# Feed-forward blocks: one more slab by seven products in three of four, and the next stage's input work pulled ahead of the weight split

## The chip, the cores and the metric

The kernel runs on one core of one Trainium2 chip, as one program. The metric is device time in microseconds (us) from one execution. Engines: TensorE (PE; its weight loads PEld), VectorE (DVE), ScalarE (ACT), GpSimd (POOL) and SyncE (SP), which issues the DMAs.

## The reference, cut to what matters

Two blocks follow one another, each two layers deep, on x of 512 tokens by 1024 channels, all float32. Each layer of the first block holds two feed-forward blocks, with a mixer (stick-breaking attention beside a gated delta rule) and a cross attention between them; the second block's layers are attention with a gated embedding.

```python
def swiglu_ffn(x, w_in, w_out):
    gate, up = jnp.split(x @ w_in, 2, axis=-1)
    return (jax.nn.silu(gate) * up) @ w_out

for l in range(DEPTH):                     # DEPTH = 2, D_FF = 2816
    h = h + 0.5 * swiglu_ffn(rms_norm(h, ffn1_norm[l]), ffn1_w_in[l], ffn1_w_out[l])
    h = h + hybrid_mixer(rms_norm(h, mix_norm[l]), ...)
    h = h + memory_cross_attention(rms_norm(h, xattn_norm[l]), rms_norm(mem, mem_norm[l]), ...)
    h = h + 0.5 * swiglu_ffn(rms_norm(h, ffn2_norm[l]), ffn2_w_in[l], ffn2_w_out[l])
```

So there are four feed-forward blocks, called here the first (ffn1 of layer 0) to the fourth (ffn2 of layer 1).

## The kernel before, in words

**Numbers in two parts.** Each float32 operand is split into a high part (rounded to the matmul's own type, made by ScalarE as a copy) and a low part (what is left, made by VectorE as a subtraction). One product of the mathematics is three matmuls: high by high, high by low, low by high (line 346).

**Slabs.** Weights stream from memory in slabs of 128 partitions. A slab of an input projection is 2048 wide and holds 8 chunks of channels for two groups of 128 output columns. Three raw buffers hold slabs; SyncE loads slab g when slab g-3 was used. ScalarE makes the high part of slab g (`high`, line 314) into one of two buffers once slab g-2 was used; VectorE makes the low part (`low`, line 321) in place. While TensorE works on slab s, the other engines prepare slab s+2 as far as they can.

**A feed-forward block** (class `Ffn`) has two halves. Each half has 11 input slabs (one hidden chunk of 128 each: a gate product and an up product) and then 8 "deep" slabs, which multiply the 11 hidden chunks by w_out into one chunk of 128 channels of h each. Input slabs are of two kinds:

- *plain*: 8 chunks by 2 outputs by 3 matmuls of 512 columns (48 matmuls). VectorE evicts both outputs times the row's norm factor (line 3523), ScalarE applies silu, VectorE multiplies (3538), ScalarE makes the high part of the hidden chunk (3430) and VectorE the low part (3541).
- *seven*: the product as 2 by 2 blocks with seven block products in place of eight (Strassen's form, Winograd's variant), 7 by 4 by 3 = 84 matmuls of 256 columns (line 3365). Its units run in the order A11, S1, S2, A12, S3, S4, A22. Before it VectorE makes three sums of weight blocks (3595 to 3600), and ScalarE and VectorE split them: `vector_first` (3605) gives the low part that A11 waits for, `vector_rests` (3611) and `vector_second` (3616) the others. During it VectorE adds partial products in a "join" (3624): unit S3 waits for the first join, unit A22 for the second.

**Blocks of x.** The sevens need x itself in blocks: seven tiles of 128x1024, from h times gain times the norm factor (`vector_row`, 3656, two rows of four instructions), four sums (3635 to 3641), seven high copies on ScalarE (3506) and seven low parts on VectorE (3647). The first A11 of a block waits for all seven low parts. Before, five slabs are plain in the second to fourth block and the work on x is spread over slabs 0 to 3 (`x_from` 0); in the first block six are plain and it is spread over slabs 1 to 4 (`x_from` 1). `vector_x(s, 0)` stands behind the slab's eviction, `vector_x(s, 1)` behind the product of silu and up.

**The slab ahead of the first seven** (`vector_enter`, evictions on line 3560) prepares slab s+2 between its own steps.

**What sets the order.** Each engine runs one fixed program, written by the loops over slabs, and stays in order; semaphores tie the engines. `tensor_plain` waits for the split slab, for two free banks of four (those of slab s-2) and in slab 0 for each chunk of the new x. The norm's matmuls (`norm_tensor`, line 464) stand in slab 0 ahead of chunk `NORM_AT`, in the first block in slab 1. `NextX` makes the next stage's x chunk by chunk from h: high (ScalarE, 415), square (422), low (VectorE, 433) and sum of squares (443). `LoadX` starts the program: it issues the loads and runs `WARM` float32 matmuls of ones (line 1076), while the first chunks of x and of slab 0 come in and are split.

Of the kernel before, what the change touches and what calls it, by code (L numbers as in the profile page):

```python
# [628 lines left out]
class Project(Stage):  # L629
# [42 lines left out]
    def scalar(self, act):  # L672
        for s, (r, i) in enumerate(self.slabs):
            for side in self.sides:
                side.scalar(act, s)
            if s == 0 and self.norm is not None:
                self.norm.norm_scalar(act)
            if len(self.jobs[s]) == 2:
                r.evac.scalar(self.k, act, self.jobs[s], 0, i)
            if (s or not self.first) and not (self.split_later and s == len(self.slabs) - 1):  # L680
                self.k.high(act, self.g0 + s + 2)
            if self.jobs[s]:
                r.evac.scalar(self.k, act, self.jobs[s], len(self.jobs[s]) - 1, i)

    def vector(self, dve):
        k = self.k
        for s, (r, i) in enumerate(self.slabs):
# [9 lines left out]
            if (s or not self.first) and not (self.split_later and s == len(self.slabs) - 1):  # L697
                k.low(dve, self.g0 + s + 2)
            if self.jobs[s]:
                r.evac.finish(k, dve, self.jobs[s], len(self.jobs[s]) - 1, i)  # L700

# [309 lines left out]
class LoadX(Stage):  # L1011

    WARM = 12
# [2174 lines left out]
class Ffn(Stage):  # L3188
# [6 lines left out]
    NORM_AT = 5  # L3195
# [3 lines left out]
    def __init__(self, k, name_at, x, gain, next_x, sides=(), first=False):  # L3199
# [5 lines left out]
        self.plain, self.x_from = (6, 1) if first else (5, 0)  # L3205
# [197 lines left out]
    def scalar(self, act):  # L3403
        k = self.k
        for s, slab in enumerate(self.slabs):
# [8 lines left out]
            if slab.kind == "plain":  # L3414
                act.wait_ge(k.bank_free, slab.jobs[0].n + 1)
                a = self.hidden(slab.j, F32)[0]
                k.nc.scalar.activation(a, a, ACT.Silu).then_inc(k.act_done, 1)
            if ahead is None:
# [12 lines left out]
            elif slab.j[1]:  # L3431
                act.wait_ge(k.bank_free, slab.jobs[0].n + 1)
                self.next_x.scalar(act, slab.j[0])
# [75 lines left out]
    def vector(self, dve):  # L3509
        k, nc = self.k, self.k.nc  # L3510
        for s, slab in enumerate(self.slabs):
# [5 lines left out]
            if now is not None and slab.kind == "plain":  # L3517
                self.vector_enter(dve, s)
                continue
            if slab.kind == "plain":  # L3520
# [7 lines left out]
            self.vector_x(dve, s, 0)  # L3528
# [13 lines left out]
            elif slab.j[1]:  # L3542
                self.next_x.vector(dve, slab.j[0])
# [83 lines left out]
    def vector_x(self, dve, s, part):  # L3627
# [9 lines left out]
        elif at == (1, 1):  # L3637
# [4 lines left out]
        rest = {(2, 0): ((self.A11, 1), (self.S3, 4)), (2, 1): ((self.S1, 5), (self.S2, 6), (self.A12, 2)),  # L3642
                (3, 0): ((self.S4, 3), (self.A22, 7))}
# [297 lines left out]
```

## Time and profile before

| | |
|---|---|
| median of 3 runs | 3074.25 us (3070.44 to 3074.66) |
| profiled execution | 3071.89 us |
| its span in the trace | 3070.1 us |
| mean granted clock of TensorE | 0.999 |
| TensorE busy | 3037.7 us, 99% of the span |
| VectorE busy | 1990.5 us, 65% |
| ScalarE busy | 1498.1 us, 49% |
| DMA | 25.1% of 16 engines, 90 GB/s |

TensorE is on nearly all of the chain that ended last (92% of it). A duration in a timeline row is an instruction's own; successive instructions of one engine overlap by some hundredths of a microsecond, so the distance between two starts is what one of them costs in a queue. A row with xN merges N instructions. The bracket behind a row is the idle time ahead of it and what ended that.

### The profile page before, as it was taken

Reading aid. Unit: us, or ns where it says so; the run is one execution under the profiler, and the core shown is the slowest. Engines: PE = TensorE matmul, PEld = TensorE weight load, DVE = VectorE, ACT = ScalarE, POOL = GpSimd, SP = SyncE. Lnnn points to the kernel's source line nnn. Section 1 sums busy time; section 2 is a strip of 40 time slices with the busy share of each in tenths; the row PEclk is TensorE's granted clock in tenths of the full one; section 3 lists DMA queues with packets and bytes.
Section 4 is the critical chain, followed back from the end, with each engine's and each line's share of the span. In section 5 each row is a group of like instructions: output and inputs, shape, how many; then the busy total and the mean of one; then the engine's idle time right before and its main releaser. Section 6 shows DMA issues by size and latency. Waiting matters only on the chain.

```text
span 3070.1 us, 45342 instructions
## 1 busy us (share of the span) xinstructions
PE 3037.7 (99%) x19178; PEld 2603.2 (85%) x19178; DVE 1990.5 (65%) x2741; ACT 1498.1 (49%) x2083; POOL 150.3 (5%) x158
## 2 busy tenths in 40 slices
PE   9999999999999999999999999999999999999999
PEld 7999887888789998989887788789998886888777
DVE  7667439855584866758447855576675568554774
ACT  5444436553453544435335653454444558454673
POOL 0000000300000000000000200000000006000150
PEclk9999999999999999999999999999999999999999
DMA  4232321132122322232221122122222220222202
GB/s 158 99 115 99 115 72 66 43 124 83 69 97 90 112 97 102 97 116 96 104 83 69 56 85 109 55 96 97 109 98 101 94 83 29 81 104 83 83 31 88
DMA packets 49545, 275.29 MB, mean 90 GB/s; under 512 B 5312, under 2 KB 8896, under 8 KB 26304
## 3 DMA queue, kind: packets, MB, share of 16 engines
q1 hardware_dynamic: 49344, 272.40, 25.1%
q8 instruction: 152, 2.49, 0.3%
q14 instruction: 49, 0.40, 0.0%
HBM read 270.28 MB, written 2.10 MB: 89 GB/s over the span
## 4 chain that ended last, share of the span: by engine, by line
PE 92%; DVE 5%; ACT 2%; issue 1%; DMA 0%; POOL 0%; DVEq 0%; SPq 0%; ACTq 0%; POOLq 0%
PE banks L346 61%; PE banks L3365 22%; PE banks L2612 1%; PE banks L2653 1%; ACT weights L2993 1%; DVE weights L3041 1%; PE banks L1682 1%; PE banks L1832 1%; PE banks L1648 0%; PE banks L1668 0%; ACT slab_hi L314 0%; DVE weights_turned L3062 0%; PE banks L1845 0%; PE banks L3784 0%; PE banks L1703 0%
## 5 line engine op out<-in xcount | busy, mean ns | idle before, releaser
L314 ACT ACTIVATE slab_hi<-slab_raw 128x2048 fp32r<-128x2048 f32 (+2 forms) x207 | 351.7, 1699 | 638.9 <-PE banks L346 615.0
L346 PE MATMUL banks<-x_hi,slab_hi 128*128 128x512 f32 x1488 | 589.1, 396 | 2.5 <-DVE x_lo L433 2.1
L346 PE MATMUL banks<-x_hi,slab_lo 128*128 128x512 f32 x1488 | 580.2, 390 | 0.0
L346 PE MATMUL banks<-x_lo,slab_hi 128*128 128x512 f32 x1488 | 580.0, 390 | 0.0
L321 DVE TENSOR_TENSOR slab_lo<-slab_raw,slab_hi 128x2048 fp32r<-128x2048 f32 (+2 forms) x203 | 409.6, 2018 | 181.6 <-ACT slab_hi L314 181.4
L3365 PE MATMUL banks<-x_blocks_hi,x_area_parts 128*128 128x256 f32 x1736 | 399.4, 280 | 0.0
L346 PE MATMUL banks<-hidden_parts,slab_hi 128*128 128x512 f32 x1280 | 394.3, 389 | 0.0
L346 PEld LDWEIGHTS banks<-x_hi,slab_hi 128*128 128x128 f32 x1488 | 279.7, 188 | 67.9 <-issue 8.7
L346 PEld LDWEIGHTS banks<-x_lo,slab_hi 128*128 128x128 f32 x1488 | 279.9, 188 | 59.5 <-issue 2.9
L346 PEld LDWEIGHTS banks<-x_hi,slab_lo 128*128 128x128 f32 x1488 | 279.6, 188 | 58.9
L3365 PE MATMUL banks<-x_blocks_hi,slab_lo 128*128 128x256 f32 x1072 | 299.2, 279 | 0.0
L3365 PEld LDWEIGHTS banks<-x_blocks_hi,x_area_parts 128*128 128x128 f32 x1736 | 296.7, 188 | 0.8 <-issue 0.5
L346 PEld LDWEIGHTS banks<-hidden_parts,slab_hi 128*128 128x128 f32 x1280 | 239.6, 188 | 49.3
L3365 PE MATMUL banks<-x_blocks_lo,x_area_parts 128*128 128x256 f32 x980 | 273.6, 279 | 0.0
L346 PE MATMUL banks<-hidden_parts,slab_lo 128*128 128x512 f32 x640 | 249.1, 389 | 0.0
L3365 PE MATMUL banks<-x_blocks_hi,slab_hi 128*128 128x256 f32 x784 | 219.5, 280 | 0.0
L3365 PE MATMUL banks<-x_blocks_lo,slab_hi 128*128 128x256 f32 x784 | 218.9, 279 | 0.0
L3365 PEld LDWEIGHTS banks<-x_blocks_hi,slab_lo 128*128 128x128 f32 x1072 | 201.3, 188 | 0.0
L3365 PEld LDWEIGHTS banks<-x_blocks_lo,x_area_parts 128*128 128x128 f32 x980 | 183.5, 187 | 0.2
L3577 DVE SCALAR_TENSOR_TENSOR h<-banks,h 128x512 f32<-128x512 f32 x64 | 44.2, 691 | 214.5 <-PE banks L346 214.5
L3365 PEld LDWEIGHTS banks<-x_blocks_hi,slab_hi 128*128 128x128 f32 x784 | 147.1, 188 | 0.2 <-issue 0.2
L3365 PEld LDWEIGHTS banks<-x_blocks_lo,slab_hi 128*128 128x128 f32 x784 | 146.8, 187 | 0.0
(458 smaller groups left out, 5466.0 us busy)
## 6 DMA issues: line engine op xcount, KB each, us to landing
slab_raw<-slabs SPq DMA_DIRECT2D x195, 1024.0 KB, 4.8
slab_raw<-slabs SPq DMA_DIRECT2D x64, 704.0 KB, 4.0
slab_raw<-slabs SPq DMA_DIRECT2D x16, 640.0 KB, 3.8
h<-xT SPq DMA_DIRECT2D x8, 256.0 KB, 5.8
memory<-memT SPq DMA_DIRECT2D x2, 1024.0 KB, 5.4
out<-h SPq DMA_DIRECT2D x7, 256.0 KB, 4.9
constants<-con SPq DMA_DIRECT2D x1, 1284.5 KB, 9.8
slab_raw<-slabs SPq DMA_DIRECT2D x4, 256.0 KB, 5.2
```

The source lines that it names most:

```text
L314: self.nc.scalar.activation(self.wh[:, g % self.HIGHS, 0:w], self.raw[:, g % self.RAWS, 0:w], ACT.Copy).then_inc(self.hi_ready, 1)
L321: self.nc.vector.tensor_tensor(self.wl[:, g % self.RAWS, 0:w], self.raw[:, g % self.RAWS, 0:w], self.wh[:, g % self.HIGHS, 0:w].bitcast(F3 ...
L346: mm = self.nc.tensor.matmul(out, left[a], right[c], start=start and n == 0, stop=stop and n == 2)
L1682: mm = nc.tensor.matmul(ps[64 * c:64 * c + 64, 2, b * P:S], v[:, b, (2 * p + c) * SB_DIM:(2 * p + c + 1) * SB_DIM], self.prob[:, at:at + n ...
L1832: mm = nc.tensor.matmul(self.product_bank(g)[rows, u - 8 * g, :], self.lm[n][rows, u, :], self.d[rows, u, :], start=True, stop=True, skip_ ...
L2612: mm = nc.tensor.matmul(self.scores_of(u), self.q[:, 2 * h + c, tb * P:(tb + 1) * P], self.kt[:, 2 * h + c, :], start=c == 0, stop=c == 1)
L2653: mm = nc.tensor.matmul(ps[:, self.out_banks[h][c], :], self.v[:, b, (2 * h + c) * P:(2 * h + c + 1) * P], self.pt[:, h % 2, b, :], start= ...
L2993: ins = nc.scalar.activation(w, w, ACT.Exp, scale=-1.0, bias=self.col(self.nm, tb, c), accum_out=self.col(self.sm, tb, c))
L3041: ins = nc.vector.tensor_tensor_reduce(self.weights(u, c)[:, at], self.bank(u, c)[:, at], self.table(u // self.UNITS)[:, S - (tb + 1) * P: ...
L3365: mm = self.k.nc.tensor.matmul(out, left[a], right[c], start=start and n + a + c == 0, stop=n == self.BLOCK - 1 and a == 1, skip_group_che ...
L3577: k.nc.vector.scalar_tensor_tensor(out=h, in0=k.ps[:, job.bank, :], scalar=0.5, in1=h, op0=ALU.mult, op1=ALU.add) \
```

## The change

Five edits:

1. `plain` goes from 5 to 4 in the second, third and fourth feed-forward block: hidden chunk 4 becomes a seven. The first block stays at 6.
2. In all four blocks `vector_x(s, 0)` stands ahead of the slab's eviction where s > `x_from`, and the seven low parts of x go over two slabs (four and three) in place of three slabs (two, three and two).
3. At a projection's last slab, and at each deep slab of the second half, the next x (high, square, low, sum) stands ahead of the split of slab s+2.
4. `NORM_AT` goes from 5 to 3.
5. `WARM` goes from 12 to 20.

```diff
--- before.py
+++ after.py
@@ -677,10 +677,13 @@
                 self.norm.norm_scalar(act)
             if len(self.jobs[s]) == 2:
                 r.evac.scalar(self.k, act, self.jobs[s], 0, i)
-            if (s or not self.first) and not (self.split_later and s == len(self.slabs) - 1):
+            last, more = s == len(self.slabs) - 1, s or not self.first
+            if more and not last:
                 self.k.high(act, self.g0 + s + 2)
             if self.jobs[s]:
                 r.evac.scalar(self.k, act, self.jobs[s], len(self.jobs[s]) - 1, i)
+            if more and last and not self.split_later:
+                self.k.high(act, self.g0 + s + 2)
 
     def vector(self, dve):
         k = self.k
@@ -694,10 +697,13 @@
                 r.evac.vector(k, dve, self.jobs[s], n, i)
                 if n == 0 and len(self.jobs[s]) == 2:
                     r.evac.finish(k, dve, self.jobs[s], n, i)
-            if (s or not self.first) and not (self.split_later and s == len(self.slabs) - 1):
+            last, more = s == len(self.slabs) - 1, s or not self.first
+            if more and not last:
                 k.low(dve, self.g0 + s + 2)
             if self.jobs[s]:
                 r.evac.finish(k, dve, self.jobs[s], len(self.jobs[s]) - 1, i)
+            if more and last and not self.split_later:
+                k.low(dve, self.g0 + s + 2)
 
     def tensor(self, pe):
         k = self.k
@@ -1010,7 +1016,7 @@
 
 class LoadX(Stage):
 
-    WARM = 12
+    WARM = 20
 
     def __init__(self, k, x, sources):
         self.k, self.x, self.sources = k, x, sources
@@ -3192,7 +3198,7 @@
 
 
     HALF, BLOCK, COLS = FC // 2, KC // 2, S // 2
-    NORM_AT = 5
+    NORM_AT = 3
     UNITS, LAST = 7, FC + KC
     A11, S1, S2, A12, S3, S4, A22 = range(UNITS)
 
@@ -3202,7 +3208,7 @@
         for side in self.sides:
             side.of = self
         at_in, at_out = name_at
-        self.plain, self.x_from = (6, 1) if first else (5, 0)
+        self.plain, self.x_from = (6, 1) if first else (4, 0)
         self.slabs = []
         self.g0 = k.claim("slab", 2 * (self.HALF + KC))
         for half in range(2):
@@ -3415,6 +3421,9 @@
                 act.wait_ge(k.bank_free, slab.jobs[0].n + 1)
                 a = self.hidden(slab.j, F32)[0]
                 k.nc.scalar.activation(a, a, ACT.Silu).then_inc(k.act_done, 1)
+            if slab.kind == "deep" and slab.j[1]:
+                act.wait_ge(k.bank_free, slab.jobs[0].n + 1)
+                self.next_x.scalar(act, slab.j[0])
             if ahead is None:
                 if self.more(s):
                     k.high(act, slab.g + 2)
@@ -3428,9 +3437,6 @@
                 else:
                     act.wait_ge(k.bank_free, slab.jobs[1].n + 1)
                 k.nc.scalar.activation(self.hidden(slab.j)[0], self.hidden(slab.j, F32)[1], ACT.Copy).then_inc(k.hh_ready, 1)
-            elif slab.j[1]:
-                act.wait_ge(k.bank_free, slab.jobs[0].n + 1)
-                self.next_x.scalar(act, slab.j[0])
             self.scalar_x(act, s, 1)
             if now is not None:
                 self.scalar_seed(act, now)
@@ -3517,6 +3523,8 @@
             if now is not None and slab.kind == "plain":
                 self.vector_enter(dve, s)
                 continue
+            if s > self.x_from:
+                self.vector_x(dve, s, 0)
             if slab.kind == "plain":
                 for job, to in zip(slab.jobs, self.hidden(slab.j, F32)):
                     dve.wait_ge(job.sem, job.value)
@@ -3525,7 +3533,10 @@
                 self.vector_hidden(dve, s)
             else:
                 self.vector_add(dve, s)
-            self.vector_x(dve, s, 0)
+                if slab.j[1]:
+                    self.next_x.vector(dve, slab.j[0])
+            if s <= self.x_from:
+                self.vector_x(dve, s, 0)
             if ahead is not None:
                 self.vector_sums(dve, ahead)
             elif self.more(s):
@@ -3539,8 +3550,6 @@
                 self.vector_x(dve, s, 1)
                 dve.wait_ge(k.hh_ready, self.n0 + slab.j + 1)
                 nc.vector.tensor_tensor(hl, product, hh.bitcast(F32), ALU.subtract).then_inc(k.hl_ready, 1)
-            elif slab.j[1]:
-                self.next_x.vector(dve, slab.j[0])
             if now is not None:
                 self.vector_join(dve, now, 0)
             if ahead is not None:
@@ -3639,8 +3648,8 @@
             nc.vector.tensor_tensor(t2, b22, t1, ALU.subtract).then_inc(self.x_made.sem, 1)
             dve.wait_ge(*self.x_made.at(5))
             nc.vector.tensor_tensor(t4, b21, t2, ALU.subtract).then_inc(self.x_made.sem, 1)
-        rest = {(2, 0): ((self.A11, 1), (self.S3, 4)), (2, 1): ((self.S1, 5), (self.S2, 6), (self.A12, 2)),
-                (3, 0): ((self.S4, 3), (self.A22, 7))}
+        rest = {(2, 0): ((self.A11, 1), (self.A12, 2), (self.S4, 3), (self.S3, 4)),
+                (2, 1): ((self.S1, 5), (self.S2, 6), (self.A22, 7))}
         for u, n in rest.get(at, ()):
             dve.wait_ge(*self.x_hi.at(n))
             dve.wait_ge(*self.x_made.at(6))
```

VectorE's program in the second feed-forward block, from slab 1's eviction on, before (`hidden<-banks` is an eviction, `x_blocks` the work on x, `slab_lo ... 128x2048` the low part of plain slab s+2):

```order
L3523 TENSOR_TENSOR hidden<-banks,rstd 128x512 x2
L3635 TENSOR_TENSOR x_blocks<-x_blocks 128x1024
L3636 TENSOR_TENSOR x_blocks<-x_blocks 128x1024
L321 TENSOR_TENSOR slab_lo<-slab_raw,slab_hi 128x2048
L3538 TENSOR_TENSOR hidden<-hidden 128x512
L3639 TENSOR_TENSOR x_blocks<-x_blocks 128x1024
L3641 TENSOR_TENSOR x_blocks<-x_blocks 128x1024
L3541 TENSOR_TENSOR hidden_parts<-hidden,hidden_parts 128x512
L3523 TENSOR_TENSOR hidden<-banks,rstd 128x512 x2
L3647 TENSOR_TENSOR x_blocks_lo<-x_blocks,x_blocks_hi 128x1024 x2
L321 TENSOR_TENSOR slab_lo<-slab_raw,slab_hi 128x2048
L3538 TENSOR_TENSOR hidden<-hidden 128x512
```

The same stretch now (lines of the changed kernel):

```order
L3644 TENSOR_TENSOR x_blocks<-x_blocks 128x1024
L3645 TENSOR_TENSOR x_blocks<-x_blocks 128x1024
L3531 TENSOR_TENSOR hidden<-banks,rstd 128x512 x2
L321 TENSOR_TENSOR slab_lo<-slab_raw,slab_hi 128x2048
L3549 TENSOR_TENSOR hidden<-hidden 128x512
L3648 TENSOR_TENSOR x_blocks<-x_blocks 128x1024
L3650 TENSOR_TENSOR x_blocks<-x_blocks 128x1024
L3552 TENSOR_TENSOR hidden_parts<-hidden,hidden_parts 128x512
L3656 TENSOR_TENSOR x_blocks_lo<-x_blocks,x_blocks_hi 128x1024 x4
L3531 TENSOR_TENSOR hidden<-banks,rstd 128x512 x2
L3604 TENSOR_TENSOR first_sums<-slab_raw 128x512
L3605 TENSOR_TENSOR slab_raw<-slab_raw 128x4x128
```

The work on x now stands ahead of each eviction, and the first seven's sums follow slab 2's eviction; the low parts of plain slab 4 are gone.

VectorE in the same block, from the last sum of the first seven (slab 5) to what its first unit waits for (`slab_lo<-slab_raw,hidden_parts`, the first of the two), before:

```order
L3600 TENSOR_TENSOR first_sums<-slab_raw,first_sums 128x512
L3538 TENSOR_TENSOR hidden<-hidden 128x512
L3541 TENSOR_TENSOR hidden_parts<-hidden,hidden_parts 128x512
L3605 TENSOR_TENSOR slab_lo<-slab_raw,hidden_parts 128x1024
L3611 TENSOR_TENSOR first_sums_parts<-first_sums,hidden_parts 128x1536
L3616 TENSOR_TENSOR slab_lo<-slab_raw,hidden_parts 128x1024
L3560 TENSOR_TENSOR hidden<-banks,rstd 128x512 x2
```

And now, for slab 4:

```order
L3609 TENSOR_TENSOR first_sums<-slab_raw,first_sums 128x512
L3549 TENSOR_TENSOR hidden<-hidden 128x512
L3656 TENSOR_TENSOR x_blocks_lo<-x_blocks,x_blocks_hi 128x1024 x3
L3552 TENSOR_TENSOR hidden_parts<-hidden,hidden_parts 128x512
L3614 TENSOR_TENSOR slab_lo<-slab_raw,hidden_parts 128x1024
L3620 TENSOR_TENSOR first_sums_parts<-first_sums,hidden_parts 128x1536
L3625 TENSOR_TENSOR slab_lo<-slab_raw,hidden_parts 128x1024
L3569 TENSOR_TENSOR hidden<-banks,rstd 128x512 x2
```

Three low parts of x now stand between the product and the first seven's own low parts.

ScalarE at the seam ahead of the second feed-forward block (last slab of the projection ahead of it), before:

```order
L314 ACTIVATE slab_hi<-slab_raw 128x2048
L415 ACTIVATE x_hi<-h,params 128x512
L422 ACTIVATE h_squares<-h 128x512
L474 ACT_TABLE_LOAD
L474 ACTIVATE rstd<-banks 128x512
```

And now:

```order
L415 ACTIVATE x_hi<-h,params 128x512
L422 ACTIVATE h_squares<-h 128x512
L314 ACTIVATE slab_hi<-slab_raw 128x2048
L474 ACT_TABLE_LOAD
L474 ACTIVATE rstd<-banks 128x512
```

The last chunk's high part and square moved ahead of the slab's high part; VectorE's side moves in the same way.

## Rows read from the trace of the kernel before

**Rows 1.** the page's first part: busy time, share of the span, instructions

```profile
PE 3037.7 (99%) x19178; PEld 2603.2 (85%) x19178; DVE 1990.5 (65%) x2741; ACT 1498.1 (49%) x2083; POOL 150.3 (5%) x158
```

**Rows 2.** chain of waits in order of time: start, us, what

```profile
8.09 18.21 PE banks L346 x72
...
76.16 49.88 PE banks L3365 x420
...
846.07 47.65 PE banks L346 x210
893.72 59.80 PE banks L3365 x504
```

**Rows 3.** waits of TensorE, whole span: us in total, times, longest

```profile
PE banks L2910 <- ACT weights_turned L3003: 9.1, 18, 0.6
...
PE banks L346 <- DVE x_lo L433: 2.1, 1, 2.1
```

**Rows 4.** timeline of TensorE from the program's start: start, us, instruction

```profile
1.10 4.92 PE L1076 MATMUL banks<-ones 128*128 128x128 f32 x24 [1.10 <-DVE ones L1059]
...
4.68 1.35 PE L1076 MATMUL banks<-ones 128*128 128x128 f32 x8
```

**Rows 5.** windows: busy us of each engine, PEclk, DMA

```profile
8.00:10.00 2.00, 1.91 (x6) 1.57 (x7) 1.51 (x3) 1.57 (x3) 0.00 (x0) 0.67 1.02 362
10.00:12.00 2.00, 2.00 (x7) 1.52 (x6) 1.86 (x4) 1.69 (x4) 0.00 (x0) 0.50 1.09 420
```

**Rows 6.** timeline of VectorE, first feed-forward's first half

```profile
19.18 5.46 DVE L443 TENSOR_TENSOR sum_of_squares<-sum_of_squares,h_squares 128x512 f32<-128x512 f32 x7
...
43.61 1.28 DVE L3523 TENSOR_TENSOR hidden<-banks,rstd 128x512 f32<-128x512 f32 x2
...
70.85 0.69 DVE L3538 TENSOR_TENSOR hidden<-hidden 128x512 f32<-128x512 f32 x1
...
81.23 0.42 DVE L3624 TENSOR_TENSOR banks<-banks,fifth_product 128x256 f32<-128x256 f32 x1
```

**Rows 7.** timeline of ScalarE, the same stretch

```profile
27.19 0.60 ACT L474 ACTIVATE rstd<-banks 128x512 f32<-128x512 f32 x1 [0.36 <-PE banks L464]
```

**Rows 8.** timeline of VectorE, second feed-forward's first half

```profile
849.63 1.30 DVE L3523 TENSOR_TENSOR hidden<-banks,rstd 128x512 f32<-128x512 f32 x2 [5.62 <-PE banks L346]
...
859.55 0.69 DVE L3523 TENSOR_TENSOR hidden<-banks,rstd 128x512 f32<-128x512 f32 x1
...
861.72 1.22 DVE L3635 TENSOR_TENSOR x_blocks<-x_blocks 128x1024 f32<-128x1024 f32 x1
...
863.99 2.28 DVE L321 TENSOR_TENSOR slab_lo<-slab_raw,slab_hi 128x2048 fp32r<-128x2048 f32 x1
...
869.19 0.68 DVE L3541 TENSOR_TENSOR hidden_parts<-hidden,hidden_parts 128x512 fp32r<-128x512 f32 x1
...
890.75 1.23 DVE L3605 TENSOR_TENSOR slab_lo<-slab_raw,hidden_parts 128x1024 fp32r<-128x1024 f32 x1 [0.26 <-ACT hidden_parts L3476]
892.12 1.76 DVE L3611 TENSOR_TENSOR first_sums_parts<-first_sums,hidden_parts 128x1536 fp32r<-128x1536 f32 x1 [0.15 <-ACT hidden_parts L3480]
...
894.94 1.28 DVE L3560 TENSOR_TENSOR hidden<-banks,rstd 128x512 f32<-128x512 f32 x2
...
898.79 0.42 DVE L3624 TENSOR_TENSOR banks<-banks,fifth_product 128x256 f32<-128x256 f32 x1
```

**Rows 9.** timeline of ScalarE, the same stretch

```profile
860.98 0.61 ACT L3417 ACTIVATE hidden<-hidden 128x512 f32<-128x512 f32 x1
861.50 1.90 ACT L314 ACTIVATE slab_hi<-slab_raw 128x2048 fp32r<-128x2048 f32 x1
```

**Rows 10.** timeline of VectorE, the seam ahead of the second feed-forward

```profile
838.44 0.69 DVE L901 SCALAR_TENSOR_TENSOR h<-banks,h 128x512 f32<-128x512 f32 x1 [2.57 <-PE banks L346]
...
843.32 0.68 DVE L443 TENSOR_TENSOR sum_of_squares<-sum_of_squares,h_squares 128x512 f32<-128x512 f32 x1
```

**Rows 11.** timeline of TensorE at the same seam

```profile
845.05 1.02 PE L464 MATMUL banks<-sum_of_squares,ones 128*128 128x512 f32 x2
```

## The prediction

> **What bounds the kernel now.** I read four views in this order. First the busy times [rows 1]: TensorE works 99% of the span, VectorE 65%, so over the whole only TensorE's own work counts. Then the chain of waits [rows 2]: the reader is to see that plain slabs and sevens follow each other as one stretch of TensorE, with nothing between. Third TensorE's list of waits [rows 3]: no line of a feed-forward block or of a seam stands in it, except one wait of 2.1 us at the start. Last the timelines of VectorE and ScalarE in the stretch that the change touches [rows 6 to 9]. The average hides what they show: ahead of a block's first seven VectorE has hardly a pause. The question is whether it can do the same work one slab earlier.
>
> Durations come from one execution of 3071.89 us (span 3070.1, so 1.8 lies around it). The median shown is 3074.25, which is 2.36 more; I add that at the end.
>
> **What a slab costs.** 210 matmuls of 512 columns take 47.65, 0.2269 each, so a plain slab of 48 takes 10.89. 504 of 256 columns take 59.80, 0.1187 each, so a seven of 84 takes 9.97 [rows 2]. Each moved slab gives 0.92, three give 2.77. Within a seven the unit S3 starts after 4 units of 12, that is 5.70 after its start.
>
> **Edits 1 and 2, second to fourth block.** TensorE would want slab 4 at 893.72 - 10.89 = 882.83. VectorE must by then have finished the first low part of slab 4's seven. In steps from slab 0's eviction at 849.63, durations being distances between starts [rows 8]:
> - to slab 1's eviction as before: 9.92 (859.55)
> - x(1, 0), two sums, now ahead of the eviction: 863.99 - 861.72 = 2.27
> - eviction 1.21 (1.30 for the pair, less overlap)
> - low part of 2048, product, two sums: 869.19 - 863.99 = 5.20
> - low part of the hidden chunk 0.61
> - four low parts of x, at 2.27 / 2 each: 4.54
> - slab 2's eviction 1.21, then the first seven's sums. From an eviction at 894.94 to the join at 898.79 are 3.85; less 1.21 this gives 2.64 for the sums
> - product 0.61, three low parts of x 3.41, hidden low part 0.61, and the seven's first low part 1.22 (890.75 to 892.12, less 0.15 idle).
>
> The sum is 33.45, done at 883.08 without a single pause. That is already 0.25 late. One pause I expect: before, ScalarE's silu starts at 860.98 and the high part of 2048 at 861.50, for 1.90, so VectorE's low part can start at 863.4 and starts at 863.99 [rows 8, 9]. Now the eviction comes 2.27 later. It ends at 859.55 + 2.27 for the first output; silu starts at about 862.5, the high part at 863.06, and it ends at 864.96. VectorE would be at its low part at 863.03, so it idles 1.97. The first low part is done at 885.05 and TensorE starts at 885.10: a stall of 2.27.
>
> A second one follows. Behind the first low part VectorE has the rest (2.82 from 892.12 to 894.94), the eviction with sums (3.85) and the join's first instruction (0.42). From the first low part's start, 883.83: 883.83 + 1.13 + 2.82 + 3.85 + 0.42 = 892.05. S3 waits for this and is wanted at 885.10 + 5.70 = 890.80: a stall of 1.30. Then both are in step, with VectorE the shorter one as in the sevens now.
>
> Per block 2.27 + 1.30 - 0.92 = 2.65, times three 7.95. What is queued behind the wait on TensorE is the whole seven, and nothing else can use the time. The bounds of this term: with the pause hidden 0.25 + 0.05 + 1.30 - 0.92 = +0.68 per block; with no stall at all -0.92; with a second such pause at slab 2 it could reach +4.6. I take 2.65, for each of its steps has a row of the same instruction.
>
> **First block, edits 2 and 5.** Plain slabs stay six. The 12 products of ones leave two records each: 24 take 4.92, 0.205 each [rows 4]. Eight more are 16 records: 3.28, ending at 6.02 + 3.28 = 9.30 at that rate. The first 16 took 3.58 (4.68 - 1.10), 0.224 each, and at half of that the addition ends at 7.81. The real work can start at 8.09 [rows 2]. Now TensorE idles 2.1 ahead of it [rows 3], and the granted clock is 0.67 and then 0.50 in the four microseconds behind [rows 5], that is down to the lower of its two levels (1.2 GHz). So the 72 matmuls take 18.21 in place of 72 x 0.2269 = 16.34. If the ones fill the gap, 1.87 are gained; but the norm's matmuls behind them need the sums of squares, which end at 19.18 + 5.46 = 24.64 [rows 6], while 72 matmuls at full speed end at 24.43. TensorE would be ahead by 26.13 - 24.70 = 1.43, the norm factor by only 0.36, since ScalarE waits just 0.36 for it (its table load is on the way) [rows 7].
>
> No row shows that the clock stays up through 8:00 to 12:00 if the ones go on; that the last eight records took 1.35, 0.169 each against 0.224, shows it rising under them [rows 4].
>
> But VectorE sets this block's first seven too. With x(2, 0) ahead of the eviction, in the same steps from slab 1's eviction at 43.61 - 0.36 = 43.25 [rows 6]: x(2, 0) to 45.52, eviction 46.73, a pause for ScalarE's high part to 48.70, 5.20 to 53.90, hidden 54.51, four low parts 59.04, eviction 60.25, high part and low part of slab 5 to 64.51. TensorE wants slab 5 at 63.84 and stalls some 0.7. Then product, three low parts, hidden low part, eviction, sums: 72.89. Before, from that point (70.85) to the join (81.23) are 10.38. Now the join ends at 72.89 + 10.38 + 0.42 = 83.69 and S3 starts at 83.74. Before, it started at 76.16 + 5.70 = 81.86. This block costs +1.88. VectorE sets it, so the warm-up's gain is lost: without it the block would be 0.36 later. Bounds: -1.43 (no stall) to +2.8 (the ones end at 9.30 and the stalls stand).
>
> **Edits 3 and 4.** At a seam TensorE waits for nothing now. The norm's matmuls at 845.05 [rows 11] move up by two chunks of six: to 842.33. The sum of squares ends at 844.00 now [rows 10], too late for that; with x in front it is h at 838.44 + 0.69 = 839.13, then high, square and sum at about 0.6 to 0.7 each, 841.1: 1.2 to spare. The split of the slab behind it comes 2.4 later but is due only at the start of slab 1, 5 us after. In the deep slabs the extra steps ahead of the split take 2 of some 7.5 us. I cost both at 0; if edit 3's cover failed, edit 4 would stall up to 1.7 per seam.
>
> **The sum.** 3071.89 + 1.88 + 7.95 = 3081.72. Plus 2.36, rounded down for the pauses that partly overlap: **3083.0**.
>
> **Rivals.**
> A, VectorE has the reserve after all, and nothing stalls: not slower. Place: the wait ahead of the first seven. It decides if the first low part is done by 882.83, that is if 33.45 + 1.97 shrink to 33.20. For it: TensorE waits nowhere in these blocks now, and VectorE is at 65%. Against it: the sum of rows is over it even without a pause. Time: -2.77 - 1.43 = -4.2, 3070.0.
>
> B, the pause of 1.97 isn't there (ScalarE's silu comes between, or other waits shift) but the work is too much: +0.68 x 3 + 1.88 = +3.9, 3078.
>
> C, the stalls bring the clock down. For it: after the one idle stretch of 2.1 us in the trace the clock went to 0.67 and 0.50 [rows 5], and 1.87 were lost. Three stalls of 2.27 could each cost up to 1.87 more; since a slower TensorE reaches S3 later, up to 1.30 of that hides in the second stall. So +0.6 to +1.9 a block, 3085 to 3089, say 3087. Against it: that idle stretch followed only 5 us of work, these follow hundreds. The Trainium skill, "TensorE: Matmul & The Clock Gate", section "Why this matters for your kernels", warns only of long idle gaps between bursts of matmuls; by that rule the three stalls would cost nothing beyond themselves and C falls away. The row at the start agrees with it only in part: there the clock fell behind a gap no longer than these.
>
> D, the longer run of ones doesn't do what it says: the clock falls all the same. That takes 0.36 off the gain as long as VectorE sets the block and 1.43 in case A (then 3071.5). Nothing in the rows excludes it; it goes with each case, and gets no chance of its own.
>
> **How the numbers follow.** A difference of 0.2% (6.1 us) is about what can be told from no change: 3068.1 to 3080.4. Forecast 0.52, own range 3079 to 3087; B 0.20; C 0.15; A 0.13. Slower takes 0.45 of the forecast, 0.05 of B and C whole: 0.65. Faster has a third of A: 0.04. The rest is 0.31. The range of 3072 to 3090 leaves out most of A and what lies above C.
>
> **What would show it.** In the profile after, VectorE idles some 2 us for the slab's high part in slab 1 of three blocks and not again up to the first seven. TensorE waits there for VectorE's low part of slab 4, about 2.3, three times, and for the join about 1.3. The first block shows stalls of 0.7, then 1 to 1.5. From 8 to 12 the granted clock is 1.00. No wait at the norm's matmuls, except at the first block. I am wrong if the first seven starts without a wait, if the waits are there but the clock in the seven behind them is under 1.00, or if a norm or a deep slab shows a wait.

## The result and the profile after

The changed kernel takes 3083.43 us (median of 6 runs, 3081.71 to 3085.5), the kernel before 3074.32 in the same comparison (3070.44 to 3075.14). The ratio is 1.0033, 95% interval 1.002 to 1.0046: slower, by 9 us. The forecast was 3083.0. That it agrees with the median to 0.4 is partly luck, for the runs of one kernel spread over 4 or more; the parts below show which terms were right by more than luck.

The page's first part of the changed kernel, span 3082.6 (before [rows 1]):

```profile
PE 3041.2 (99%) x19302; PEld 2611.1 (85%) x19302; DVE 2004.4 (65%) x2759; ACT 1505.3 (49%) x2098; POOL 150.3 (5%) x158
```

The shares are those of before. The reader who looks only here finds nothing. TensorE's waits do show it (us in total, times, longest); none of these lines was in the list of before:

```profile
PE banks L3371 <- DVE slab_lo L3614: 7.8, 4, 2.3
...
PE banks L3371 <- DVE banks L3633: 2.4, 2, 1.2
...
PE banks L346 <- DVE slab_lo L321: 0.7, 1, 0.7
```

Line 3371 is the seven. `slab_lo L3614` is the low part of its first unit, `banks L3633` the join ahead of S3. Each wait of three blocks for the low part is 2.35, and the fourth, in the first block, is 0.77. S3 waits 1.25 in the first block, 1.12 in the second and not at all in the third and fourth. The start's wait of 2.1 [rows 3] is gone from the list, and the windows that showed the clock's fall [rows 5] now read 1.00 in the column PEclk, the third from the right:

```profile
8.00:10.00 2.00, 2.00 (x13) 1.74 (x13) 1.75 (x4) 1.86 (x3) 0.00 (x0) 1.00 1.00 344
10.00:12.00 2.00, 2.00 (x11) 1.65 (x10) 0.98 (x3) 0.94 (x2) 0.00 (x0) 1.00 1.10 425
```

VectorE in the second block (timeline: start, us, instruction, idle ahead), which answers to [rows 8]:

```profile
853.51 1.30 DVE L3531 TENSOR_TENSOR hidden<-banks,rstd 128x512 f32<-128x512 f32 x2 [5.08 <-PE banks L346]
...
865.70 1.28 DVE L3531 TENSOR_TENSOR hidden<-banks,rstd 128x512 f32<-128x512 f32 x2
868.89 2.29 DVE L321 TENSOR_TENSOR slab_lo<-slab_raw,slab_hi 128x2048 fp32r<-128x2048 f32 x1 [1.91 <-ACT slab_hi L314]
...
887.70 1.22 DVE L3614 TENSOR_TENSOR slab_lo<-slab_raw,hidden_parts 128x1024 fp32r<-128x1024 f32 x1
...
895.49 0.42 DVE L3633 TENSOR_TENSOR banks<-banks,fifth_product 128x256 f32<-128x256 f32 x1
```

From the first eviction to the end of the seven's first low part are 888.92 - 853.51 = 35.41; the prediction had 33.45 + 1.97 = 35.42. The one pause behind the first eviction is 1.91, for ScalarE's high part. The same pause is found in the first block, twice.

Where TensorE's time went can be read off the chain of waits, by the start of the first 264 matmuls behind each block's first sevens (start, us, what). After:

```profile
128.56 59.87 PE banks L346 x264
...
960.09 59.87 PE banks L346 x264
...
1306.69 59.87 PE banks L346 x264
...
2135.92 59.87 PE banks L346 x264
```

Before, the same places:

```profile
126.04 59.87 PE banks L346 x264
...
953.52 59.87 PE banks L346 x264
...
1297.32 59.87 PE banks L346 x264
...
2123.58 59.87 PE banks L346 x264
```

The offsets are +2.52, +6.57, +9.37, +12.34. Taking off what each block starts with (0, 3.88, 6.46, 9.40, from the same chain), the four blocks cost 2.52, 2.69, 2.91 and 2.94. The forecast had 1.88 and three times 2.65. The step from 2.52 to 3.88 lies between the blocks, in the gated delta rule's stage, and steps of this size come and go there with the code unchanged (run 11).

### The profile page after: what moved, and what is told of

Same layout as the page of the kernel before. It is cut to its first block, busy times and chain, and to the rows that moved or that the text cites. A ratio compares the mean times of both kernels' runs of the same rounds, so it can differ in the third digit from the quotient of the medians.

```text
span 3082.6 us, 45635 instructions
## 1 busy us (share of the span) xinstructions
PE 3041.2 (99%) x19302; PEld 2611.1 (85%) x19302; DVE 2004.4 (65%) x2759; ACT 1505.3 (49%) x2098; POOL 150.3 (5%) x158
## 4 chain that ended last, share of the span: by engine, by line
PE 86%; DVE 9%; ACT 3%; issue 2%; DMA 0%; SPq 0%; DVEq 0%; POOL 0%; ACTq 0%; POOLq 0%
PE banks L346 54%; PE banks L3371 22%; PE banks L2618 1%; PE banks L2659 1%; DVE x_blocks_lo L3656 1%; ACT slab_hi L314 1%; ACT weights L2999 1%; DVE weights L3047 1%; PE banks L1688 1%; DVE x_blocks L3665 1%; PE banks L1838 1%; DVE hidden L3531 0%; DVE slab_lo L321 0%; PE banks L1654 0%; PE banks L1674 0%
## 5 line engine op out<-in xcount | busy, mean ns | idle before, releaser
L346 PE MATMUL banks<-x_hi,slab_hi 128*128 128x512 f32 x1440 | 569.9, 396 | 1.2 <-DVE slab_lo L321 0.7
L346 PE MATMUL banks<-x_hi,slab_lo 128*128 128x512 f32 x1440 | 560.9, 389 | 0.0
L346 PE MATMUL banks<-x_lo,slab_hi 128*128 128x512 f32 x1440 | 560.8, 389 | 0.0
L3371 PE MATMUL banks<-x_blocks_hi,x_area_parts 128*128 128x256 f32 x1772 | 408.9, 279 | 0.0
L3371 PE MATMUL banks<-x_blocks_hi,slab_lo 128*128 128x256 f32 x1120 | 314.2, 281 | 0.0
L3371 PE MATMUL banks<-x_blocks_hi,slab_hi 128*128 128x256 f32 x868 | 243.4, 280 | 0.0
L3371 PE MATMUL banks<-x_blocks_lo,slab_hi 128*128 128x256 f32 x868 | 242.3, 279 | 0.0
L3371 PEld LDWEIGHTS banks<-x_blocks_hi,slab_lo 128*128 128x128 f32 x1120 | 211.8, 189 | 0.0
L3371 PEld LDWEIGHTS banks<-x_blocks_hi,slab_hi 128*128 128x128 f32 x868 | 162.8, 188 | 0.7 <-issue 0.7
L3371 PEld LDWEIGHTS banks<-x_blocks_lo,slab_hi 128*128 128x128 f32 x868 | 162.6, 187 | 0.0
```

Source lines behind the costliest of these rows:

```text
L346: mm = self.nc.tensor.matmul(out, left[a], right[c], start=start and n == 0, stop=stop and n == 2)
L3371: mm = self.k.nc.tensor.matmul(out, left[a], right[c], start=start and n + a + c == 0, stop=n == self.BLOCK - 1 and a == 1, skip_group_che ...
```

## The experiments

In every run a block's cost is the shift of TensorE against the first profile of before between that block's beginning and the end of its first sevens, as just shown. That is finer than the medians: runs of one kernel differ by 4 to 9 us, in good part for a reason that comes last. Ratios are to the kernel before on the same chip, with 95% intervals.

**1. Five plain slabs in the three blocks, all else changed.**

```diff
-        self.plain, self.x_from = (6, 1) if first else (4, 0)
+        self.plain, self.x_from = (6, 1) if first else (5, 0)
```

> The changed kernel with five plain slabs again in the second to fourth block; everything else as changed. My theory (VectorE is late for a seven that comes one slab sooner; with five plain slabs it has a slab of TensorE's time more) expects no wait ahead of the first seven in these three blocks, though VectorE's pause of about 1.9 in slab 1 stays, and the loss of the first block alone: before + 2.4, 3076.7, some 6.7 under the changed kernel. The rival (the order of x ahead of the evictions costs by itself in every block) expects stalls there too and 3080 or more.

Measured: 3076.83, ratio 1.0014 (1.0005 to 1.0023). Blocks +2.47, +0.82, +0.79, +0.77. No wait ahead of a later block's first seven. But S3 waits in all four:

```profile
PE banks L3371 <- DVE banks L3633: 3.3, 4, 1.2
```

So the first seven's stall comes from taking a slab away. Edit 2 costs by itself as well, 0.8 per block, where I had expected nothing, and the four blocks together lose 4.85 where I had expected 2.4 (that the median is near the 3076.7 expected is chance: before ran at 3071.75 beside it). VectorE now pauses 1.9 for ScalarE's high part in slab 1 and again in slab 2, and its join starts at 901.82, 3.03 later than before, while TensorE is only 2.23 later there. S3 had 0.2 to spare [rows 2, 8] and cannot absorb that. Whether the order of x or the gathering of its low parts in two slabs weighs more was not separated.

**2. Evictions ahead of x again, four plain slabs.**

```diff
-            if s > self.x_from:
-                self.vector_x(dve, s, 0)
...
-            if s <= self.x_from:
-                self.vector_x(dve, s, 0)
+            self.vector_x(dve, s, 0)
```

> The changed kernel with the work on x behind the eviction in every slab, as before; four plain slabs and the low parts of x over two slabs stay. My theory expects VectorE's pauses of 1.9 to go in all four blocks, the stall ahead of the three first sevens to fall from 2.35 to 0.3 to 0.5, that at S3 to stay at 1.1 to 1.3, and the first block to lose under 0.5: 3074.3 + 3 x (0.4 + 1.2 - 0.92) = 3076.3, 7 under the changed kernel. The rival (VectorE's amount of work alone sets it, the pause is time that it has anyway) expects the stalls as they are and 3083.

Measured: 3080.65, ratio 1.0025 (1.0016 to 1.0034). Blocks -1.46, +3.52, +3.54, +3.53. My expectation was wrong: in the first block it came, and more (-1.46, the ones included), in the others the stall grew to 2.93. The pauses show why (VectorE's timeline):

```profile
859.38 0.69 DVE L3529 TENSOR_TENSOR hidden<-banks,rstd 128x512 f32<-128x512 f32 x1 [0.88 <-PE banks L346]
...
870.26 0.69 DVE L3529 TENSOR_TENSOR hidden<-banks,rstd 128x512 f32<-128x512 f32 x1 [1.52 <-PE banks L346]
```

The pause of 1.91 for ScalarE is gone, but the eviction that now stands in front waits for TensorE to end the slab, twice, 2.40 together. These two pauses are those of the kernel before, to the hundredth, as its own timeline has them between the rows of [rows 8]: 0.88 ahead of slab 1's second eviction, and

```profile
872.00 0.69 DVE L3523 TENSOR_TENSOR hidden<-banks,rstd 128x512 f32<-128x512 f32 x1 [1.52 <-PE banks L346]
```

The wait at S3 that I had expected did not show. Behind each of the three stalls the granted clock fell (0.65 and 0.50 in the two windows from 884 to 888, second block), so TensorE came to S3 later. For four plain slabs the changed order is the better of the two, by 0.6 to 0.8 a block; a part of that can be the clock, which fell in all three blocks here and in two of three there.

**3. The seams and the norm alone** (edits 3 and 4 on the kernel before; the projections' part of edit 3 goes in as in the change's diff).

```diff
-    NORM_AT = 5
+    NORM_AT = 3
...
+            if slab.kind == "deep" and slab.j[1]:
+                act.wait_ge(k.bank_free, slab.jobs[0].n + 1)
+                self.next_x.scalar(act, slab.j[0])
```

> The kernel before with edits 3 and 4 alone: the next x ahead of the split at the seams, and the norm ahead of chunk 3. My theory costs them at nothing: no wait at the norm, none at a deep slab, 3074.3 within 1. The rival (the split that now comes later is late for the slab behind the seam) expects a wait of TensorE for a slab's low part, 0.5 or more at each of some seams, 3076 or more.

Measured: 3072.17 against 3071.75, ratio 1.0001 (0.9992 to 1.001). Blocks 2 to 4: within 0.02 of nothing; no wait at a norm or deep slab of the later blocks. Costed rightly at nothing.

**4. Twenty products of ones alone**, on the kernel before.

```diff
-    WARM = 12
+    WARM = 20
```

> The kernel before with 20 products of ones in place of 12. The granted clock stays at 1.00 in the first 12 us and TensorE is some 1.4 earlier at the first norm. My theory expects VectorE to give nearly all of this back at the first seven's S3, where the join ends only 0.2 before TensorE wants it: a gain of 0.2 to 0.4, 3074.0. The rival (TensorE's lead lasts) expects 1.4 to 1.9 less than before: 3072.6.

Measured: 3070.85, ratio 0.9994 (0.9985 to 1.0002), which the timing cannot tell from no change. In the trace the first block is 1.33 earlier than in the first profile of before, and the lead lasts to the block's end: the rival was right on that. How much of it the ones give is less sure, since the same code as before was 0.87 earlier in one execution (run 11). VectorE's evictions had waited for TensorE there, by this row and one like it at 54.44 in the trace of before:

```profile
65.32 0.69 DVE L3523 TENSOR_TENSOR hidden<-banks,rstd 128x512 f32<-128x512 f32 x1 [0.51 <-PE banks L346]
```

An earlier TensorE lets VectorE go earlier too, so the slack of 0.2 at S3 is not used up. In this profile the lead is lost behind the block, in the gated delta rule's stage (1.34, granted clock 0.57 from 604 to 608, as in run 11), and both spans are 3070.1.

**5. Each part of the work on x one place earlier**, evictions in front, and ScalarE's high copies of x with them; the first block as before, edits 3 to 5 as changed.

```diff
+            if s == 0 and not self.first:
+                self.vector_row(0)
...
+            steps = {(0, 0): 1, (0, 1): 2, (1, 0): 3}
+            rest = {(1, 1): ((self.A11, 1), (self.A12, 2), (self.S4, 3), (self.S3, 4)),
+                    (2, 1): ((self.S1, 5), (self.S2, 6), (self.A22, 7))}
```

> Four plain slabs in three blocks, evictions ahead of x, and in these three blocks each part of the work on x one place earlier: the first row ahead of slab 0's eviction, where VectorE idles 5.08 and the norm factor is ready 3.5 before it, then row, sums, sums, four low parts in slab 1 and three in slab 2. The first block has its order of before; edits 3 to 5 as changed. My theory, corrected by the last runs (an eviction cannot run before TensorE ends its slab, and the first seven's sums cannot before slab 2 ends at 875.9 in the changed kernel's clock): behind that point 0.61 + 2.64 + 0.61 + 3.41 + 0.61 + 1.22 = 9.1, done at 885.0, TensorE wants it at 886.7: no stall; the join ends at 892.0 and S3 is wanted at 892.4: none. So three times -0.92 and a little from the ones: before - 3. The rival (VectorE's amount of work ahead of the first seven sets it, wherever it stands) expects the stalls of about 3 per block to stay, before + 6 to 8.

Measured: 3070.43 against 3072.36, ratio 0.9988 (0.9979 to 0.9997): faster than before. Blocks -1.03, -0.50, -0.58, -0.54. The row of x stands in the pause ahead of the first eviction:

```profile
844.84 2.74 DVE L3674 SCALAR_TENSOR_TENSOR x_blocks<-h,params,rstd 128x512 f32<-128x512 f32 x4 [1.56 <-ACT rstd L479]
848.29 1.37 DVE L3534 TENSOR_TENSOR hidden<-banks,rstd 128x512 f32<-128x512 f32 x2 [0.71 <-PE banks L346]
```

The same four plain slabs, the same work, and no stall ahead of the first seven; S3 keeps 0.31 each, where I had expected none, so a block gains 0.5 to 0.6 and not 0.92. So the amount of work was not the bound. What bound was that it stood behind waits.

**6. ScalarE's high part ahead of silu**, all else changed.

```diff
+                if ahead is None and self.more(s):
+                    k.high(act, slab.g + 2)
                 act.wait_ge(k.bank_free, slab.jobs[0].n + 1)
...
-                if self.more(s):
+                if self.more(s) and slab.kind != "plain":
                     k.high(act, slab.g + 2)
```

> The changed kernel, but ScalarE makes a plain slab's next high part ahead of silu in place of behind it, so that VectorE's low part needn't wait for it. My theory (the pause of 1.91 in slab 1, two of them in the first block, passes on to the first seven in full) expects 3 x 1.9 + 2.3 less than the changed kernel: its stalls 3.5 per block fall to 1.6, the first block loses under 0.5, before + 2.5. The rival (the pause is only changed into a wait for TensorE's evictions, as in the run with the evictions ahead) expects the stalls of 2.35 to stay above 2, and under 2 gained.

Measured: 3073.21 against 3072.36, ratio 1.0 (0.9991 to 1.0009). Blocks -2.61, +0.84, +0.88, +0.85. Waits:

```profile
PE banks L3371 <- DVE banks L3635: 3.0, 3, 1.0
...
PE banks L3371 <- DVE slab_lo L3616: 1.4, 3, 0.5
```

This is the cleanest test of the forecast's main step. The pause is gone from the second block's timeline, the stall ahead of the first seven falls from 2.35 to 0.47, by the 1.9 of the pause, and the one at S3 stays at 1.01. The pause is not VectorE's spare time. No fall of the clock follows these shorter stalls.

**7. The first block in its order of before**, all else changed.

```diff
-            if s > self.x_from:
+            if s > self.x_from and not self.first:
...
-            if s <= self.x_from:
+            if s <= self.x_from or self.first:
...
+        if self.first:
+            rest = {(2, 0): ((self.A11, 1), (self.S3, 4)), (2, 1): ((self.S1, 5), (self.S2, 6), (self.A12, 2)),
+                    (3, 0): ((self.S4, 3), (self.A22, 7))}
```

> The changed kernel with the order of before in the first block alone (x behind the evictions, low parts over three slabs). My theory: the first block's three stalls (0.74, 0.77, 1.25) go, about 2.4 less than the changed kernel, and the three others stay as they are. The rival (they come from the longer run of ones, or TensorE's lead only turns into another wait) expects the sum of that block's waits to stay above 1.5.

Measured: 3080.12, ratio 1.002 (1.0011 to 1.0029). Blocks -1.58, +2.72, +2.98, +2.97. All waits of the first block are gone, which is 4.1 against the changed kernel; I had expected 2.4, and left out that the ones' 1.4 comes through once VectorE no longer sets the block.

**8. The norm at 3 alone**, on the kernel before.

```diff
-    NORM_AT = 5
+    NORM_AT = 3
```

> The kernel before with NORM_AT 3 alone, the next x still behind the split. My theory: the last sum of squares ends at 844.00 in the trace of before, and TensorE now wants it at 842.33, so it waits 1.7 at each of three seams, 5 in all, and nothing later gives it back: before + 5. The rival (TensorE's norm may come late, but the norm factor and the first evictions come no later than before, and banks are free) says the same stall is there but 1 or more is given back at a later wait: before + 2 or less.

Measured: 3078.84, ratio 1.002 (1.001 to 1.0029). The later blocks' shift is +1.88, +1.84, +1.84; TensorE waits at each seam:

```profile
PE banks L464 <- DVE sum_of_squares L443: 4.7, 3, 1.6
```

Edit 3 is thus what makes edit 4 free. Nothing is given back: the shift is some 0.3 above the wait of 1.57 each.

**9. As 5, with the sum for t2 between the two evictions of slab 1.**

```diff
+                    if s == n == 1 and not self.first:
+                        self.vector_t2(dve)
```

> The run with x one place earlier, and the sum for t2 moved in between the two evictions of slab 1, where VectorE idled 1.26 for TensorE. My theory expects the whole chain behind it 1.1 earlier, the 0.31 wait at S3 gone, and so 0.92 gained per block in place of 0.55: before - 1.3 (the ones) - 2.8 = before - 4.1. The rival (the wait at S3 is set by what stands behind the first seven's sums, which wait for slab 2's end anyway) expects the 0.31 to stay and before - 3.

Measured: 3068.8 against 3073.31, ratio 0.9985 (0.9976 to 0.9994), the fastest of all by its blocks (the two ratios' intervals, of 5 and 9, overlap). Blocks -1.22, -1.11, -1.14, -1.15. The wait at S3 is gone, and VectorE's timeline shows t2 where the pause was:

```profile
857.68 0.68 DVE L3536 TENSOR_TENSOR hidden<-banks,rstd 128x512 f32<-128x512 f32 x1
858.29 1.21 DVE L3673 TENSOR_TENSOR x_blocks<-x_blocks 128x1024 f32<-128x1024 f32 x1
859.63 0.69 DVE L3536 TENSOR_TENSOR hidden<-banks,rstd 128x512 f32<-128x512 f32 x1
```

A block gains 1.12, and not 0.92, because the price of the added seven was taken too high. Nothing waits here, and seven sevens take (chain of waits)

```profile
881.36 69.57 PE banks L3371 x588
```

against 59.80 for six before [rows 2]: 9.77 for the one more, where a plain slab takes 10.89. The forecast's 9.97 was the average of the six, which holds some 0.4 of short losses: the sevens of the second half run at 108.83 for 924, 0.1178 each, and those six at 0.1187.

**10. The changed kernel with 12 products of ones.**

```diff
-    WARM = 20
+    WARM = 12
```

> The changed kernel with 12 products of ones again. The prediction said that VectorE sets the first block and the ones give it 0.36 at most; with the ones alone the kernel of before gained 1.3 in its trace. My theory: in the changed kernel ScalarE's table load and VectorE's chain behind it start at the same time with either number, so the first block ends within 0.4 of where it ends now (first deep slab at 128.4). The rival (the ones' 1.3 comes through here as well) expects it at 129.7.

Measured: 3083.81, ratio 1.0033 (1.0022 to 1.0044). First block +2.44, where the changed kernel has +2.52: the ones give nothing there in these two executions. ScalarE's table load stands directly ahead of the norm factor, with no wait for TensorE, in the changed kernel itself:

```profile
25.98 1.28 ACT L474 ACT_TABLE_LOAD   x1
27.27 0.60 ACT L474 ACTIVATE rstd<-banks 128x512 f32<-128x512 f32 x1
```

The other blocks are +2.73, +2.91 and +2.71, and only in the third, of +2.91, did the clock fall behind the stall (0.50 and 0.65 in its windows).

**11. The kernel before once more, one profile** (no edit).

> The kernel before, unchanged, profiled once more. It is to show whether the granted clock's falls in the gated delta rule's stage (none in the first profile of before, one of 1.3 to 1.6 in others) come and go with the same code. If so: the trace up to 550 as in the first profile within 0.5, and a fall in one of its two stages or in none. The rival (the falls belong to the edits) expects none in either stage.

Measured: 3074.27. The first block is 0.87 earlier than in the first profile, outside the 0.5 that I had expected: TensorE idled 1.69 at the start and the clock did not fall behind it. In the gated delta rule's stage 3.36 are lost that the first profile does not lose (us, busy per engine, granted clock in the third column from the right):

```profile
602.00:606.00 4.00, 3.67 (x34) 3.42 (x33) 1.72 (x4) 0.59 (x1) 0.00 (x0) 0.65 0.00 0
606.00:610.00 4.00, 4.00 (x26) 3.78 (x25) 0.00 (x0) 0.60 (x1) 0.00 (x0) 0.50 0.01 4
```

The first profile of before in the same stretch:

```profile
602.00:606.00 4.00, 3.67 (x61) 3.41 (x59) 2.31 (x5) 1.08 (x2) 0.00 (x0) 1.00 0.00 0
606.00:610.00 4.00, 4.00 (x43) 3.81 (x42) 1.76 (x4) 0.60 (x1) 0.00 (x0) 1.00 0.01 4
```

Same code, another clock. The changed kernel's step in that stage is such a fall (0.72 from 606 to 610): 1.60 within it, of which 0.24 are given back before the second block. That stage stands in both layers. The first layer's lost 1.3 to 3.4 in 6 of the 13 profiles, the second's 1.6 to 3.0 in 4.

## Why the prediction was right, and where its steps were off

**VectorE late for the first seven, second to fourth block.** Right in mechanism and place, and close in size. The stall is 2.35 three times (2.27 forecast), S3's 1.12 in the second block (1.30), the pause 1.91 (1.97). Run 6 shows that the pause passes on in full, run 1 that the missing slab makes the stall. Net 2.69 to 2.94 a block for 2.65. That the second block came within 0.04 is luck in part, for its terms err both ways: the moved seven gives 1.12 and not 0.92 (run 9), and 2.35 + 1.12 - 1.12 leaves 0.34 of the 2.69 in short losses of the sevens behind, which the forecast had at nothing and which I did not trace.

**The rows added up, the reading of the pauses did not.** The forecast said that ahead of the first seven VectorE has hardly a pause. The trace of before has one of 5.62 ahead of slab 0's eviction [rows 8], and behind it 0.88, 1.52 and 0.51 for TensorE and 0.96 for ScalarE up to the seven's low part. The forecast also treated the new pause as a consequence of x standing ahead of the eviction, and I then took the old order for the cure. Run 2 refutes this: the other order has its own, longer pauses, on TensorE. What cures it is work put into the pauses (5, 9) or the awaited step put ahead (6).

**First block.** Forecast +1.88, measured +2.52. Of the missing 0.64, the part in the norm factor is 0.44: it starts at 27.27, not 0.36 earlier than 27.19 [rows 7]. This is chance and no fault of the term. The whole chain ahead of the norm factor starts 0.44 later, with a load that came in 0.44 later. ScalarE's timeline, before and after:

```profile
15.81 2.01 ACT L282 ACTIVATE slab_hi<-slab_raw 128x1024 fp32r<-128x1024 f32 x2 [1.32 <-DMA slab_raw<-slabs]
```

```profile
16.25 2.01 ACT L282 ACTIVATE slab_hi<-slab_raw 128x1024 fp32r<-128x1024 f32 x2 [1.30 <-DMA slab_raw<-slabs]
```

The kernel before has it at 16.26 in run 11, and over all profiles it lies between 15.53 and 16.59. From it to the norm factor are 11.02 in the changed kernel and in runs 4, 10 and 11, and 11.38 in the first profile of before, so the 0.36 was there to be had: in run 4, with the load at 15.78, the norm factor starts at 26.80. The rest, 0.2, are short losses in the sevens behind. One step of the recorded sum is off by 0.1 (from 64.51 its steps lead to 72.99 and not to 72.89), which changes nothing here. That VectorE sets this block and swallows the ones was right (runs 7 and 10).

**Seams and norm.** 0 forecast, 0 measured (run 3). The price if the cover failed was put at 1.7 per seam; without it the wait is 1.57 and the shift 1.84 to 1.88 (run 8).

**The rivals.** A (nothing stalls) is ruled out for this order, but run 9 reaches it with the same work, and run 5 nearly: the sum of rows said how late VectorE would be in this order, not that four plain slabs were impossible. B's stalls are those of run 6: +0.86 a block for +0.68. D fell away, since the clock stayed at 1.00 from 8 to 12. C's mechanism came about in two of three blocks, and with it one of the signs that I had named for being wrong, a clock under 1.00 in the seven behind a stall: it fell in the third and the fourth block and not in the second. The windows of the third block, changed kernel:

```profile
1235.00:1237.00 2.00, 1.56 (x9) 1.59 (x10) 2.00 (x3) 0.00 (x0) 0.00 (x0) 0.71 0.93 393
1237.00:1239.00 2.00, 2.00 (x11) 2.00 (x11) 2.00 (x3) 0.63 (x2) 0.00 (x0) 0.50 0.14 57
```

The second block, at the same distance behind its stall:

```profile
889.00:891.00 2.00, 1.94 (x17) 1.97 (x18) 2.00 (x2) 0.30 (x1) 0.00 (x0) 1.00 0.91 381
891.00:893.00 2.00, 2.00 (x20) 2.00 (x19) 2.00 (x4) 0.71 (x3) 0.00 (x0) 1.00 0.04 8
```

But it costs 0.2 (2.91 and 2.94 for 2.69), not the 0.6 to 1.9 that I had put on it: TensorE at half speed reaches S3 later, and would have waited there anyway, and S3's 1.12 is missing from the list in just these two blocks. The same blocks of runs 7 and 10 bear this out, with the same stall: 2.91 to 2.98 in the three with a fall, 2.71 to 2.73 in the three without. The Trainium skill ("TensorE: Matmul & The Clock Gate", section "Why this matters for your kernels") warns of long idle gaps between bursts of matmuls, as what brings the clock down. The traces agree only in part, since stalls of one and the same length (about 2.35) were followed by a fall in five blocks of nine and not in the others.

**The sum.** 9.83 were forecast between the profiled executions. Measured are 12.4 (3084.29 for 3071.89): 1.36 more by the chance fall in the delta rule's stage, 0.64 by the first block, and 0.59 by the three others. In medians it is 9.1, since other executions of before have such a fall too. I had taken the first profile of before, with none in that stage, as typical, and added 2.36 for its distance to the median without knowing what that was. The sum was then 3084.08, and the 1.08 taken off it "for the pauses that partly overlap" have no row behind them. The match to 0.4 is luck to that extent.

## What to carry to other kernels

When a helper of the bounding engine gets a deadline one stage sooner, add its queue up in rows from the last point where it idled to the deadline, pauses included; shares of busy time say nothing. Then look what each pause waits for: moving work past a wait often trades it for a wait on another engine, while filling the pause, or putting the awaited step ahead on its own engine, removes it. Compare kernels that differ by a few microseconds by the shift of the bounding engine between landmarks of the traces, not by their medians alone.

## What was not expected of the hardware

Behind the idle stretch at the program's start the clock fell in three profiles (idle 2.06, 2.35 and 2.17, in before and runs 8 and 10) and not in two with 1.69 and 1.70 (runs 11 and 3). Behind the 2.93 of run 2 it fell three times in three. Behind the short waits of the delta rule's stage (0.2 to 0.9 each) it fell in some executions of the same code and not in others, which costs 1.3 to 3.4. Much of the spread between runs goes with the clock: of 82 executions of the kernel before beside runs 1 to 11, the 20 with a mean granted clock of 1.000 took 3067.8 to 3071.7, and the 10 with 0.997 took 3076.3 to 3077.0. What decides whether it falls stays open.

In run 6 the matmuls of 256 columns in the first block went faster than anywhere else, at the same granted clock: 282 in 32 us, where the kernel before has 273.

```profile
91.00:123.00 32.00, 31.98 (x282) 31.78 (x281) 24.23 (x31) 14.60 (x23) 0.00 (x0) 1.00 0.22 79
```

Before:

```profile
91.00:123.00 32.00, 32.00 (x273) 31.99 (x273) 25.24 (x32) 15.67 (x24) 0.00 (x0) 1.00 0.24 79
```

This gives 1.3 of that block's -2.61 and has nothing to do with the edit as far as the runs show; no other profile repeats it (270 to 274 in those 32 us), and its cause is open.
